# Reading and writing the fp32r products of a two-layer encoder from the last column to the first

## The chip, the cores and the metric

The kernel runs on one core of a Trainium2 chip. The metric is the device time of one execution in microseconds. It is measured in several runs, of which the median is given; a separate execution is taken with the hardware profiler.

## The reference: one step of a hybrid streaming encoder

Two layers work on a prompt of 2048 tokens and on 8 sample streams of 16 tokens, all with a model width of 1024 and in 32-bit floats.

```
p = rmsnorm(x) @ w_in[l]          # 1024 x 3584: mixer a | b | c | cross-attn q | gate
layer 0: softmax attention over the own chunk of 64 and 8 chunks before, with a bias by distance
layer 1: HGRN2 gated linear recurrence, state 128 x 128 for each of 6 heads
every layer: 4-head cross-attention into 256 memory tokens
y = concat(mixer_out, cross_out) * silu(gate);   x = x + y @ w_out[l]     # 1024 x 1024
final rmsnorm
```

Besides the two activations, the kernel returns the newest keys and values, the recurrent states and the memory keys and values. The largest part of the arithmetic is `rmsnorm(x) @ w_in[l]` for 2176 tokens, twice; then comes `y @ w_out[l]`.

## The kernel before, in words

**Products from high and low parts.** A plain fp32 product is one kind of matmul here, an fp32r product another. Where the kernel uses fp32r, it splits each operand into a high part (the value cast to fp32r) and a low part (the value minus its high part, again fp32r), and adds three products: weights' low by data's high, weights' high by data's high, weights' high by data's low.

**The input projection** (`project`, from L967; its tensor part is L1458 to L1480). The contraction over 1024 channels is cut into two halves of four blocks of 128, the output channels into pairs of groups of 128, and the tokens into two halves. Of these two-by-two blocks, seven sums or differences are formed (a scheme with seven products in place of eight), the *terms* j = 0 to 6. One term is 12 matmuls into one PSUM bank, `BANK[j]`: four of the weights' low part (L1464), then eight of the high part with the data's high and low parts in turn (L1468). The weights are the stationary operand (128 x 128), the data is the moving one. There are 14 column pairs of the weights, seven terms for each, and four passes over the tokens. A pass has 512 tokens, so the moving operand has 256 columns; the first pass also carries the 128 sample tokens, and its moving operand has 320. In layer 1, the first two column pairs of pass 0 are made with plain fp32 matmuls (L1459, four for a term).

TensorE goes through the steps in a fixed order written out by hand. Before a term it waits for the weights' low part from VectorE (`w.s_lo`), and for the bank to have been emptied (`s_cp`, `s_cb`). ScalarE makes the weights' high part (L509), VectorE the low part (L516); ScalarE copies (L1204, L1207) and VectorE combines (L1307) the banks into the output once the last matmul of a term has signalled `s_mm`. The weight terms of passes 1 to 3 are fetched again from memory by SyncE.

**The band attention of layer 0** (`prompt_band`, from L1927) works tile by tile on 128 tokens with plain fp32 matmuls for scores (L2321), transposes (L2352) and values (L2408). The output projection is woven between them by an inner function `project` (L2439 to L2455): for each tile and each half of 512 output columns it adds 8 x 3 fp32r matmuls (L2453). Here the data `yh`, `yl` is the stationary operand and the weights `woh`, `wol` are the moving one, with 512 columns.

**The recurrence of layer 1** (`prompt_hgrn`, from L2771) has the same output projection (L3032 to L3049), with its three products on lines L3043, L3044 and L3047, among plain fp32 products of 32 to 256 columns and transposes. A tile's 48 output products are given out in pieces between the levels of the recurrence.

Before the first projection stands `begin` (memory keys and values, with 64 plain fp32 matmuls of 512 columns at L942); between the recurrence and the second projection stands the sample streams' part. All moving operands and outputs of matmuls are read and written with a step of +1 column.

Of the kernel before, what the change touches and what calls it, by code (L numbers as in the profile page):

```python
# [22 lines left out]
KD = D // P  # L23
# [27 lines left out]
def place(step):  # L51
    p, r = divmod(step, STEPS)
    c, j = divmod(r, TERMS)
    return p, c, j
# [14 lines left out]
def made(step):  # L69

    return step + 1 - TERMS * place(step)[0]
# [34 lines left out]
def keep_going(nc, bank, ident, n):  # L106

    for _ in range(n):
        nc.tensor.transpose(bank[:, 0:P], ident[:], ident[:])
# [857 lines left out]
def project(nc, l, sem, ps_in, v, x, w, x_of, proj, keep, room, early, samp, opening):  # L967
# [30 lines left out]
    def pair(step):  # L998
        return step // TERMS
# [26 lines left out]
    with ExitStack() as ctx:  # L1026
# [18 lines left out]
        BANK = [B1[:], B52[:, 1], B4[:], B52[:, 0], B3[:], B76[:, 1], B76[:, 0]]  # L1045
# [26 lines left out]
        with nc.Block() as block:  # L1072
# [336 lines left out]
            @block.tensor  # L1409
            def _(pe):  # L1410
                def turn(i, kh):
                    pe.wait_ge(s_xn, i + 1)
                    if i or kh:
                        pe.wait_ge(x.s_raw, RAWS + 2 * i + kh)
                    elif l:
                        pe.wait_ge(x.s_raw, RAWS)
                        pe.wait_ge(s_rawa, len(ON_ACT))
                    for k in range(4):
                        at = (4 * kh + k) * P
                        ins = nc.tensor.transpose(TP[:, k * P:(k + 1) * P], nat[i % 2][:, at:at + P], ident[:])  # L1420
                    ins.then_inc(s_tp, 1)
                def first_turn(n):
                    i, kh = TURNS[n]
                    pe.wait_ge(early.s_xn, i + 1)
                    if n == 8:
                        pe.wait_ge(x.s_raw, 2)
                    if n == 9:
                        pe.wait_ge(x.s_raw, 3)
                    for k in range(4):
                        at = (4 * kh + k) * P  # L1430
                        ins = nc.tensor.transpose(SPACE[n % 8][:, k * P:(k + 1) * P], early.x[i][:, at:at + P], ident[:])
                    ins.then_inc(s_tp, 1)
                if l:
                    for n in range(len(TURNS)):
                        first_turn(n)
                    pe.wait_ge(x.s_raw, 5)
                    keep_going(nc, SPACE[3], ident, 9)
                for step in range(ALL):
                    p, c, j = place(step)
                    q, n = pair(step), x.width(p)  # L1440
                    if step < w.whole:
                        if j in w.PLAIN:
                            w.loaded(pe, c)
                        else:
                            w.summed(pe, c, j)
                        if c == 0 and j in x.SUMS:
                            pe.wait_ge(x.s_add, x.MADE[0][j])
                    else:
                        if not kept(step):
                            pe.wait_ge(w.s_lo, made(step) - w.whole)  # L1450
                        if c == (w.whole // TERMS if p == 0 else 0):
                            pe.wait_ge(x.s_lo, TERMS * p + (list(LOWS.values()).index(j) if l and p == 0 else j) + 1)
                    if j == 0 or j == 3:
                        wait(pe, s_cp, 3 * (q - 1) + (1 if j == 0 else 3))
                    if q and j:
                        pe.wait_ge(s_cb, 4 * (q - 1) + (2, 1, 2, 3, 4, 4)[j - 1])
                    if step < w.whole:
                        for k in range(4):  # L1458
                            ins = nc.tensor.matmul(BANK[j][:, 0:n], w.source(step)[:, k], x.source(0, j)[:, k],  # L1459
                                                   start=(k == 0), stop=(k == 3))  # L1460
                        ins.then_inc(s_mm, 1)
                        continue
                    for k in range(4):
                        ins = nc.tensor.matmul(BANK[j][:, 0:n], w.lo[j][:, k], x.of(x.hi, p, j)[:, k], start=(k == 0), stop=False)  # L1464
                    ins.then_inc(w.s_free, 1)
                    for k in range(4):
                        for i, y in enumerate((x.hi, x.lo)):
                            ins = nc.tensor.matmul(BANK[j][:, 0:n], w.hi[j][:, k], x.of(y, p, j)[:, k],  # L1468
                                                   start=False, stop=(k == 3 and i == 1))
                    ins.then_inc(s_mm, 1)  # L1470
                    if p < PASSES - 1 and c in (2, 4, 6, 8) and j in (1, 5):
                        turn(4 * p + c // 2 - 1, j // 4)
                if l == 0:
                    pe.wait_ge(x.s_raw, RAWS + 8 * (PASSES - 1))
                    keep_going(nc, TP, ident, 14)
# [451 lines left out]
def prompt_band(nc, l, sem, sb_in, sb_far_in, ps_in, v, early, opening):  # L1927
# [24 lines left out]
    with ExitStack() as ctx:  # L1952
# [3 lines left out]
        wol = sb("pb_wol", [P, KD, D], F32R)  # L1956
# [7 lines left out]
        woh = sb("pb_woh", [P, KD, D], F32R)  # L1964
# [17 lines left out]
        yh = [sb("pb_yh0", [P, KD, P], F32R), yh1]  # L1982
        with ExitStack() as over:
            y = [sb_in(over)("pb_y0", [P, KD, P]), y1]
        yl = [sb("pb_yl0", [P, KD, P], F32R), yl1]
# [34 lines left out]
        def group_of(T, p):  # L2020

            return p if T else (p - XP) % KD
# [25 lines left out]
        def sum_of(job, half):  # L2048

            return SC[0][:, 0:512] if (job, half) == (NT, 1) else OP[:]  # L2050
# [28 lines left out]
        with nc.Block() as block:  # L2079
# [168 lines left out]
            def _(pe):  # L2248
# [190 lines left out]
                def project(job, first, last):  # L2439

                    for n in range(first, last):
                        c, part = divmod(n, 3)
                        half, k = divmod(c, KD)
                        if part == 0 and k == 0 and (job, half) != (NT, 1):
                            wait(pe, s_xadd, 2 * job + half)
                        if part == 0 and k % 4 == 0:
                            pe.wait_ge(s_yh, 2 * job + k // 4 + 1)
                        if part == 2 and k % 4 == 0:
                            pe.wait_ge(s_yl, 2 * job + k // 4 + 1)
                        if job == 0 and part == 0 and half == 0:  # L2450
                            pe.wait_ge(s_wl, FIRST.index(group_of(0, k)) + 1)
                        cs = slice(half * 512, half * 512 + 512)
                        ins = nc.tensor.matmul(sum_of(job, half), (yl if part == 2 else yh)[job % 2][:, k],  # L2453
                                               (wol if part == 1 else woh)[:, group_of(job, k), cs],
                                               start=(k == 0 and part == 0), stop=(k == KD - 1 and part == 2))  # L2455
                        if k == KD - 1 and part == 2:
                            ins.then_inc(s_op, 1)
# [22 lines left out]
                for u in range(PAIRS, U_ALL, 2):  # L2480
                    T, p = step(u)
# [289 lines left out]
def prompt_hgrn(nc, l, sem, sb_in, ps_in, v, o_s, woh, wol, wor, ahead):  # L2771
# [19 lines left out]
    with ExitStack() as ctx:  # L2791
        sb, ps = sb_in(ctx), ps_in(ctx)
        q, f, k, tT, gt, xq, masks = ahead.q, ahead.f, ahead.k, ahead.vT, ahead.gate, ahead.xq, ahead.own
# [18 lines left out]
        y = [sb(f"hg_y{i}", [P, 512]) for i in range(2)]  # L2812
        yh = sb("hg_yh", [P, KD, P], F32R)
        yl = sb("hg_yl", [P, KD, P], F32R)
# [35 lines left out]
        def sum_of(job, half):  # L2850

            return SC[bank(NT - 1, LEVELS - 1)] if (job, half) == (JOBS - 1, 0) else OP
# [4 lines left out]
        with nc.Block() as block:  # L2857
# [100 lines left out]
            def _(pe):  # L2958
# [73 lines left out]
                def project(job, first, last):  # L3032

                    for c in range(first, last):
                        half, s = divmod(c, KD)
                        to = sum_of(job, half)
                        if s == 0:
                            wait(pe, s_xadd, 2 * job if job == JOBS - 1 else 2 * job + half)
                        if s % 4 == 0:
                            pe.wait_ge(s_yh, 2 * job + s // 4 + 1)  # L3040
                        cs = slice(half * 512, half * 512 + 512)
                        g = GROUPS[s]
                        nc.tensor.matmul(to[:], yh[:, s], woh[:, g, cs], start=(s == 0), stop=False)  # L3043
                        nc.tensor.matmul(to[:], yh[:, s], wol[:, g, cs], start=False, stop=False)  # L3044
                        if s % 4 == 0:
                            pe.wait_ge(s_yl, 2 * job + s // 4 + 1)
                        ins = nc.tensor.matmul(to[:], yl[:, s], woh[:, g, cs], start=False, stop=(s == KD - 1))  # L3047
                        if s == KD - 1:
                            ins.then_inc(s_op, 1)  # L3049

# [441 lines left out]
```

## Time and profile before

| what | value |
|---|---|
| median of 3 runs | 2377.52 us |
| lowest and highest | 2376.17, 2381.19 us |
| profiled execution, span from first to last instruction | 2376.1 us |
| PE (TensorE matmuls) busy | 2312.2 us, 97% |
| PEld (weight loads) busy | 2094.7 us, 88% |
| DVE (VectorE) busy | 1819.5 us, 77% |
| ACT (ScalarE) busy | 1413.5 us, 59% |
| POOL (GpSimd) busy | 381.0 us, 16% |
| matmuls | 23787 |
| mean granted TensorE clock | 0.997 |

For the profiled execution the span stands alone; the time around it isn't recorded separately. A matmul's recorded duration reaches from its start to its modelled end, and the next one starts before that end. So the rate of a stream of matmuls is read from the distance of their starts, not from their mean duration.

### The profile page before, as it was taken

The numbers are of one execution on the slowest core, as the hardware profiler recorded it, in microseconds if no ns is written. First come the engines' busy times: TensorE is split into PE (matmuls) and PEld (weight loads), VectorE is DVE, ScalarE is ACT, GpSimd is POOL, SyncE is SP. The second block draws the span as 40 slices with busy tenths as digits, with TensorE's granted clock in tenths as the row PEclk, the third lists the DMA queues.
The fourth block names the chain that finished last, engine by engine and source line by source line (L and its number), as shares of the span: only waits on it lengthen the run. The fifth ranks groups of instructions, "written<-read, shape, count | busy, mean of one in ns | idle before, by whom it ended". The sixth has DMA issues, their size and how long they took to land. (4 is left out here: it accounts for less than half of the span.)

```text
span 2376.1 us, 61711 instructions
## 1 busy us (share of the span) xinstructions
PE 2312.2 (97%) x23787; PEld 2094.7 (88%) x23787; DVE 1819.5 (77%) x3555; ACT 1413.5 (59%) x3281; POOL 381.0 (16%) x585
## 2 busy tenths in 40 slices
PE   7999999999989999999999999999999989999998
PEld 4999999999967888888887999999999978888886
DVE  7889788887666656666666998797888777888885
ACT  4564666755565555555554564776757566666664
POOL 2332000000022221211112332000000112112111
PEclk9999999999999999999999999999999999999999
DMA  6886887769894222222226897886879793444442
GB/s 227 298 299 219 301 281 231 247 220 332 232 307 121 83 66 89 90 69 83 73 81 232 272 303 242 256 275 214 266 248 312 230 269 117 129 131 122 137 135 70
DMA packets 396664, 469.64 MB, mean 198 GB/s; under 512 B 39860, under 2 KB 248556, under 8 KB 396376
## 3 DMA queue, kind: packets, MB, share of 16 engines
q1 hardware_dynamic: 379832, 406.02, 54.4%
q0 software_dynamic: 14704, 54.92, 6.6%
q10 hardware_dynamic: 1840, 4.75, 0.7%
q8 instruction: 193, 3.16, 0.5%
q14 instruction: 95, 0.78, 0.1%
HBM read 318.77 MB, written 151.56 MB: 198 GB/s over the span
## 5 line engine op out<-in xcount | busy, mean ns | idle before, releaser
L1468 PE MATMUL pj_acc<-x_lo,pj_wh 128*128 128x256 f32 (+1 forms) x3080 | 780.9, 284 | 0.0
L1468 PE MATMUL pj_acc<-x_hi,pj_wh 128*128 128x256 f32 (+1 forms) x3080 | 780.8, 284 | 0.0
L1468 PEld LDWEIGHTS pj_acc<-x_hi,pj_wh 128*128 128x128 f32 x3080 | 578.4, 188 | 0.0
L1468 PEld LDWEIGHTS pj_acc<-x_lo,pj_wh 128*128 128x128 f32 x3080 | 578.4, 188 | 0.0
L509 ACT ACTIVATE pj_wh<-pj_wt 128x512 fp32r<-128x512 f32 x676 | 420.3, 634 | 255.9 <-DMA pj_wt<-tsum 175.1
L516 DVE SCALAR_TENSOR_TENSOR pj_wl<-pj_wt,pj_wh 128x512 fp32r<-128x512 f32 x676 | 467.0, 708 | 87.0 <-ACT pj_wh L509 79.3
L1464 PE MATMUL pj_acc<-x_hi,pj_wl 128*128 128x256 f32 (+1 forms) x3080 | 509.4, 287 | 13.8 <-DVE pj_wl L516 11.9
L1464 PEld LDWEIGHTS pj_acc<-x_hi,pj_wl 128*128 128x128 f32 x3080 | 425.3, 188 | 22.1 <-DVE pj_wl L516 19.5
L1307 DVE TENSOR_TENSOR pj_out<-pj_out,pj_acc 128x512 f32<-128x512 f32 (+1 forms) x448 | 320.8, 716 | 103.3 <-PE pj_acc L1468 69.7
L2541 DVE COPY pb_pt<-pb_SCTP 128x256 f32<-128x256 f32 (+2 forms) x266 | 115.8, 435 | 147.5 <-PE pb_SCTP L2352 74.3
L2676 ACT ACTIVATE pb_se<-pb_se,pb_mn 128x640 f32<-128x640 f32 (+4 forms) x208 | 154.6, 745 | 114.6 <-DVE pb_mn L2524 114.3
L2683 ACT COPY pb_pt<-pb_SCTP 128x384 f32<-128x384 f32 (+2 forms) x272 | 106.3, 391 | 123.7 <-PE pb_SCTP L2356 62.9
L2524 DVE CUSTOM_DVE_ANT_0 pb_se<-pb_SCTP,pb_bias 128x640 f32<-128x640 f32 (+4 forms) x204 | 137.6, 727 | 44.0 <-PE pb_SCTP L2321 38.8
L2352 PE MATMUL pb_SCTP<-ident,pb_se 128*128 128x128 f32 x1020 | 156.9, 276 | 3.9 <-ACT pb_se L2676 2.6
L2352 PEld LDWEIGHTS pb_SCTP<-ident,pb_se 128*128 128x128 f32 x1020 | 121.5, 140 | 38.5 <-issue 9.2
L1204 ACT COPY pj_out<-pj_acc 128x512 f32<-128x512 f32 (+1 forms) x112 | 68.5, 611 | 115.5 <-PE pj_acc L1468 107.2
L1207 ACT COPY pj_out<-pj_acc 128x256 f32<-128x256 f32 (+1 forms) x224 | 85.4, 381 | 73.5 <-PE pj_acc L1468 69.7
L2453 PE MATMUL pb_OP<-pb_woh,pb_yh 128*128 128x512 f32 x264 | 127.1, 481 | 0.0
L2230 POOL TENSOR_TENSOR pb_gate<-pb_gate,pb_pt 128x128 f32<-128x128 f32 x136 | 74.9, 551 | 259.6 <-DVE pb_pt L2541 259.6
L3043 PE MATMUL hg_OP<-woh,hg_yh 128*128 128x512 f32 x264 | 115.5, 438 | 0.0
L478 POOL TENSOR_TENSOR pj_wt<-pj_wraw 128x512 f32<-128x512 f32 x56 | 89.1, 1594 | 120.4 <-PE pj_acc L1464 86.5
L2321 PEld LDWEIGHTS pb_SCTP<-pb_k,pb_q 64*128 64x128 f32 x1152 | 86.0, 187 | 23.9 <-issue 11.6
(371 smaller groups left out, 3992.1 us busy)
## 6 DMA issues: line engine op xcount, KB each, us to landing
pj_wt<-tsum SPq DMA_DIRECT2D x546, 256.0 KB, 3.8
proj<-pj_out SPq DMA_DIRECT2D x112, 512.0 KB, 4.2
tsum<-pj_wt SPq DMA_DIRECT2D x140, 256.0 KB, 3.2
pj_wraw<-in_w_in_dram POOLq DMA_DIRECT2D x24, 1024.0 KB, 6.6
tsum<-pj_wraw SPq DMA_DIRECT2D x56, 256.0 KB, 4.2
hg_x<-x_mid SPq DMA_DIRECT2D x17, 512.0 KB, 3.7
pb_gate<-proj SPq DMA_DIRECT2D x16, 512.0 KB, 5.1
pb_x<-in_x_prompt_dram SPq DMA_DIRECT2D x16, 512.0 KB, 3.8
```

The source lines that it names most:

```text
L509: nc.scalar.mul(self.hi[j][:], self.source(step), scale_of(column(step // TERMS), self.l)).then_inc(self.s_hi, 1)
L516: nc.vector.scalar_tensor_tensor(out=self.lo[j][:], in0=self.source(step), scalar=scale_of(column(step // TERMS), self.l), in1=self.hi[j][ ...
L1307: nc.vector.tensor_tensor(to, to, what, op).then_inc(s_cb, 1)
L1464: ins = nc.tensor.matmul(BANK[j][:, 0:n], w.lo[j][:, k], x.of(x.hi, p, j)[:, k], start=(k == 0), stop=False)
L1468: ins = nc.tensor.matmul(BANK[j][:, 0:n], w.hi[j][:, k], x.of(y, p, j)[:, k], start=False, stop=(k == 3 and i == 1))
L2352: ins = nc.tensor.transpose(to[:, at:at + P], se[u % 2][h][:, i * P:(i + 1) * P], ident[:])
L2453: ins = nc.tensor.matmul(sum_of(job, half), (yl if part == 2 else yh)[job % 2][:, k], (wol if part == 1 else woh)[:, group_of(job, k), cs] ...
L2524: nc.vector.tensor_tensor_reduce(se[u % 2][h][:, 0:n * P], scores_at(u, h, 0, n), add, 1.0, 3e38, ALU.add, ALU.min, mn[:, at:at + 1]).then ...
L2541: ins = nc.vector.tensor_copy(pt[u % 2][h][:, low * P:low * P + width], turned_to(u, h)[:, 512:512 + width])
L2676: nc.scalar.activation(se[u % 2][h][:, 0:n], src, ACT.Exp, bias=mn[:, at:at + 1], scale=-1.0, accum_out=tot[:, at:at + 1]).then_inc(s_exp, 1)
L2683: nc.scalar.copy(pt[u % 2][h][:, 0:at], turned_to(u, h)[:, 0:at]).then_inc(s_eva, 1)
L3043: nc.tensor.matmul(to[:], yh[:, s], woh[:, g, cs], start=(s == 0), stop=False)
```

## The change

In each fp32r product, the moving operand and the output get `::-1` on their columns. The column n - 1 is read first and written first to place n - 1 of the bank, column 0 last. The stationary operand, the order of the products, the waits and the signals are the same, and so are the plain fp32 products and transposes.

```diff
                     for k in range(4):
-                        ins = nc.tensor.matmul(BANK[j][:, 0:n], w.lo[j][:, k], x.of(x.hi, p, j)[:, k], start=(k == 0), stop=False)
+                        ins = nc.tensor.matmul(BANK[j][:, 0:n][:, ::-1], w.lo[j][:, k], x.of(x.hi, p, j)[:, k, ::-1], start=(k == 0), stop=False)
                     ins.then_inc(w.s_free, 1)
                     for k in range(4):
                         for i, y in enumerate((x.hi, x.lo)):
-                            ins = nc.tensor.matmul(BANK[j][:, 0:n], w.hi[j][:, k], x.of(y, p, j)[:, k],
+                            ins = nc.tensor.matmul(BANK[j][:, 0:n][:, ::-1], w.hi[j][:, k], x.of(y, p, j)[:, k, ::-1],
                                                    start=False, stop=(k == 3 and i == 1))
...
-                        ins = nc.tensor.matmul(sum_of(job, half), (yl if part == 2 else yh)[job % 2][:, k],
-                                               (wol if part == 1 else woh)[:, group_of(job, k), cs],
+                        ins = nc.tensor.matmul(sum_of(job, half)[:, ::-1], (yl if part == 2 else yh)[job % 2][:, k],
+                                               (wol if part == 1 else woh)[:, group_of(job, k), cs][:, ::-1],
                                                start=(k == 0 and part == 0), stop=(k == KD - 1 and part == 2))
...
-                        nc.tensor.matmul(to[:], yh[:, s], woh[:, g, cs], start=(s == 0), stop=False)
-                        nc.tensor.matmul(to[:], yh[:, s], wol[:, g, cs], start=False, stop=False)
+                        nc.tensor.matmul(to[:, ::-1], yh[:, s], woh[:, g, cs][:, ::-1], start=(s == 0), stop=False)
+                        nc.tensor.matmul(to[:, ::-1], yh[:, s], wol[:, g, cs][:, ::-1], start=False, stop=False)
                         if s % 4 == 0:
                             pe.wait_ge(s_yl, 2 * job + s // 4 + 1)
-                        ins = nc.tensor.matmul(to[:], yl[:, s], woh[:, g, cs], start=False, stop=(s == KD - 1))
+                        ins = nc.tensor.matmul(to[:, ::-1], yl[:, s], woh[:, g, cs][:, ::-1], start=False, stop=(s == KD - 1))
```

## Rows read from the trace of the kernel before

**Rows 1.** The page: span, busy times, busy tenths by slice, chain.

```profile
span 2376.1 us, 61711 instructions
PE 2312.2 (97%) x23787; PEld 2094.7 (88%) x23787; DVE 1819.5 (77%) x3555; ACT 1413.5 (59%) x3281; POOL 381.0 (16%) x585
...
PE   7999999999989999999999999999999989999998
...
PE hg_OP L3043 3%; PE hg_OP L3044 2%; PE hg_OP L3047 2%; PE hg_SC L2991 2%; PE hg_SC L3115 1%; PE hg_OB L3106 1%; PE hg_OB L3107 1%; PE hg_OB L3078 1%; PE hg_SC L3058 1%; PE hg_TP L3068 1%; PE hg_TP L3025 1%; PE hg_SC L3001 0%; PE hg_TP L3090 0%; PE hg_TP L3014 0%; PE hg_SC L2996 0%
```

**Rows 2.** Windows: us, then each engine's busy us and instructions, clock, DMA.

```profile
core 0: us, PE busy (x) PEld busy (x) DVE busy (x) ACT busy (x) POOL busy (x), PEclk, DMA share, GB/s
420.00:480.00 60.00, 60.00 (x532) 60.00 (x531) 49.74 (x81) 42.52 (x93) 5.64 (x4) 1.00 0.80 254
120.00:180.00 60.00, 60.00 (x415) 59.97 (x414) 52.94 (x76) 36.22 (x75) 21.09 (x18) 1.00 0.89 297
840.00:900.00 60.00, 60.00 (x562) 50.02 (x562) 36.14 (x94) 31.06 (x82) 12.44 (x29) 1.00 0.30 89
2220.00:2280.00 60.00, 59.23 (x1147) 49.17 (x1146) 48.68 (x122) 39.40 (x114) 13.42 (x19) 1.00 0.46 136
...
51.60:647.90 596.30, 591.59 (x4800) 587.43 (x4801) 482.11 (x721) 355.64 (x708) 73.03 (x65) 1.00 0.83 266
1283.90:1887.60 603.70, 595.46 (x4744) 581.97 (x4744) 521.50 (x788) 389.41 (x762) 66.68 (x62) 1.00 0.81 262
```

**Rows 3.** Groups by form, PE alone, windows 420:480 and 120:180.

```profile
L1420 PE MATMUL pj_tp<-ident,pj_nat 128*128 128x128 f32 x20 | 3.0, 272 | 0.0
...
L1420 PE MATMUL pj_tp<-ident,pj_nat 128*128 128x128 f32 x16 | 2.4, 272 | 0.0
```

**Rows 4.** Timeline of fp32r products: start us, duration us, engine, line, count.

```profile
100.12 0.75 PE L1464 MATMUL pj_acc<-x_hi,pj_wl 128*128 128x320 f32 x4
100.70 0.31 PE L1468 MATMUL pj_acc<-x_hi,pj_wh 128*128 128x320 f32 x1
...
501.36 0.62 PE L1464 MATMUL pj_acc<-x_hi,pj_wl 128*128 128x256 f32 x4
...
501.81 0.28 PE L1468 MATMUL pj_acc<-x_hi,pj_wh 128*128 128x256 f32 x1
...
2002.48 0.48 PE L3043 MATMUL hg_OP<-woh,hg_yh 128*128 128x512 f32 x1
2002.80 0.40 PE L3044 MATMUL hg_OP<-wol,hg_yh 128*128 128x512 f32 x1
...
2003.27 0.40 PE L3043 MATMUL hg_OP<-woh,hg_yh 128*128 128x512 f32 x1
2003.50 0.40 PE L3044 MATMUL hg_OP<-wol,hg_yh 128*128 128x512 f32 x1
2003.74 0.40 PE L3047 MATMUL hg_OP<-woh,hg_yl 128*128 128x512 f32 x1
```

**Rows 5.** Waits of PE in the two projections: total us, times, longest us.

```profile
PE pj_acc L1464 <- DVE pj_wl L516: 4.4, 10, 1.5
...
PE pj_acc L1464 <- DVE pj_wl L516: 7.5, 12, 1.5
```

**Rows 6.** Groups by form, whole span: the changed products with their counts.

```profile
L1468 PE MATMUL pj_acc<-x_hi,pj_wh 128*128 128x256 f32 x2352 | 564.5, 277 | 0.0
...
L1464 PE MATMUL pj_acc<-x_hi,pj_wl 128*128 128x256 f32 x2352 | 369.9, 279 | 3.8 <-DVE pj_wl L516 3.3
...
L1468 PE MATMUL pj_acc<-x_hi,pj_wh 128*128 128x320 f32 x728 | 216.3, 309 | 0.0
...
L2453 PE MATMUL pb_OP<-pb_woh,pb_yh 128*128 128x512 f32 x264 | 127.1, 481 | 0.0
...
L3044 PE MATMUL hg_OP<-wol,hg_yh 128*128 128x512 f32 x264 | 104.3, 395 | 0.5 <-issue 0.5
```

**Rows 7.** Timeline of plain fp32 products and transposes.

```profile
27.19 12.18 PE L942 MATMUL bg_kv<-bg_wkvb,bg_xT 128*128 128x512 f32 x28
...
1286.22 2.05 PE L1459 MATMUL pj_acc<-x_raw,pj_wt 128*128 128x320 f32 x7
...
2001.69 1.04 PE L3068 MATMUL hg_TP<-ident,hg_se 128*128 128x128 f32 x8
```

## The prediction

> **What bounds the kernel now.** I began with the page's first two parts [rows 1]: PE is busy for 2312.2 of 2376.1 us (97%), DVE for 77%, ACT for 59%, and PE's row of slices shows 9 in nearly all of them. Since matmuls are pipelined and their ends are modelled, that share alone doesn't show that PE is at its peak, so the next view is the busy time by windows [rows 2]. Of 60 us in the later passes of the first projection, PE shows 60.00 and issues 532 matmuls. The list by form for that window gives 20 of them as transposes [rows 3]. At 0.109 us each (below) these take 2.2 us, so the other 512 start every 57.8 / 512 = 0.113 us. The timeline shows the same without averaging: four products from 501.36 to 501.81, 0.1125 us each [rows 4]. A product of 320 columns, in a projection's first pass, starts every (100.70 - 100.12) / 4 = 0.145 us; by the window at 120 us, (60 - 16 x 0.109) / 399 = 0.146 us [rows 2 to 4]. A product of 512 columns in an output projection starts 0.23 to 0.24 us after the one before (2003.27, 2003.50, 2003.74) [rows 4]. So in the two projections, 596.3 and 603.7 us long [rows 2], PE is fed all the time: it idles for 596.3 - 591.6 = 4.7 and 603.7 - 595.5 = 8.2 us there, nearly all of it for the low part that DVE makes [rows 5]. The band attention stage also shows PE at 60.00 of 60, and the recurrent stage at 59.23 [rows 2]. The chain that ended last, as far as the page follows it, consists of PE work, with the three output product lines at its head [rows 1]. TensorE's granted clock is 1.00 in these stretches, the level of 2.4 GHz. Every nanosecond added to a changed product is therefore paid nearly in full.
>
> **The change part by part.** Nothing is added, removed or moved: 10,824 matmuls keep their place, size, stationary operand, waits and increments. 7056 of them have 256 columns (2352 at L1464, two times 2352 at L1468), 2184 have 320 (three times 728), 1584 have 512 (three times 264 at L2453, and 264 each at L3043, L3044, L3047) [rows 6]. Two things differ per product: the order in which the columns of the moving operand are read, and the order in which the results are written. Both are turned the same way, so each value lands where it landed, and the vector and scalar engines read the banks as before. They start when the last product of a term has ended, so which column came last is nothing to them. The next product into the same bank also runs backwards, so the time between two accumulations into one column stays one interval. At equal rate the sum is 10,824 x 0 = 0.
>
> The price of a backward stream is in no row, since every pattern here goes forward. The nearest rows bound it. *Upper end:* a changed product moves one column in 0.113 / 256 = 0.44 ns, against 1 / 2.4 = 0.42 ns for a column per clock. The plain fp32 products take twice that: 28 products of 512 columns in 12.18 us, less the last one's 0.59, are 11.59 / 27 = 0.429 us each, and seven of 320 columns in 2.05 us, less 0.43, are 0.270 us, so 0.84 ns per column. Even a 128-column fp32 transpose takes (1.04 - 0.27) / 7 = 0.109 us, which is 0.85 ns per column [rows 7]. So the fp32r stream moves two neighbouring columns in the time that the plain one needs for one. If the pairing worked only upwards, 256 columns would take 0.215 us, 320 0.270, 512 0.429. That is 7056 x 0.102 = 720 us, 2184 x 0.124 = 271 us, 1584 x (0.429 - 0.232) = 312 us; sum 1303 us, less the 12.9 us that PE idles in the projections and would no longer: +1290 us. *Lower end:* a changed product has a remainder over its columns at 0.417 ns: 6.2 ns at 256, 12.7 at 320 (146 - 133.3), 18.7 at 512 (232 - 213.3). The plain ones have about 2 ns (109 - 106.7 at 128; 429.3 - 426.7 = 2.6 at 512). Were the surplus of about 4, 10 and 16 ns due to the direction, turning it round could give back 7056 x 4 + 2184 x 10 + 1584 x 16 ns = 28 + 22 + 25 = 75 us, and no more.
>
> I take zero. Both numbers of the bounds belong to something that the direction doesn't touch by necessity: a backward stream still asks for neighbours one after the other, the counts 256, 320 and 512 are even, so the pairs (255, 254), (253, 252), ... are the very pairs of the forward stream, and each lies in the same aligned 8 bytes. I choose the nearest row, the same product forward.
>
> The trace has the forward rate of 0.44 ns per column for unit steps alone [rows 4]. The Trainium skill (Advanced Engine Details and Errata, PSUM Cachelines) has the results' memory work in lines of two FP32 values, and says that every two consecutive elements should be contiguous, but also that any non-contiguous pattern significantly slows down matmuls. By its first half the reversed write costs nothing (each line is met twice in a row), and the sum is 0; read to the letter, a step of -1 is not a contiguous pattern, which speaks against this change, and the sum is at the upper end. No run yet shows which. The same page (VectorE Performance Modes) counts +1 and -1 alike as unit step for that engine; no row here shows a step of -1 on any.
>
> What is hidden if the upper end holds: DVE and ACT would have more time per term, and the waits for the low part would go; nothing else could cover PE, which has no other idle time.
>
> **The rivals.**
>
> *Pairing only upwards* (slower). Place: every fp32r product, on the read or the write side, one being enough. Price: as above, 2377.5 + 1290 = 3667 us. It decides as soon as the pair's address is formed by adding to the first rather than by recognising the line. For it: fp32r is visibly a special fast path, twice the plain rate [rows 4, 7], and special paths tend to have narrow conditions. Against it: the pairs are aligned and their members adjacent in time.
>
> *A small cost or loss per product* (slower). The path works backwards, but each stream loses something at its start, or the surplus of 4, 10 and 16 ns doubles: between 10,824 x 0.44 ns = 4.8 us, from where it can be told, and 75 us: 2382 to 2453 us. One period at 1.2 GHz, 0.83 ns, per product would be 9 us, 2386 us. For it: what happens around a product's start does cost something: the first 512-column product after plain fp32 ones is followed after 0.32 us instead of 0.23 (2002.48 to 2002.80) [rows 4]. Against it: that price is one of changing the kind of product, which stays as it is.
>
> *The surplus shrinks* (faster). If forward streams lose their 4 to 16 ns to meeting the weight loads' reads, which run all the time in the projections (PEld 60.00 of 60 in the window at 420 us [rows 2]), a backward one may meet them less: down to 2377.5 - 75 = 2302 us. For it: the surplus grows with the columns and the plain products lack it. Against it: nothing says that the direction matters.
>
> *The change does nothing* because both turns cancel before they reach the engine, as the instruction could be given forward with the same meaning. The time is then 2377.5 us and cannot be told from my forecast by time.
>
> **How the numbers follow.** The sum is 0 on the profiled execution's span of 2376.1 us; the median of the runs, 2377.52, lies 1.4 us above it and the runs spread from 2376.17 to 2381.19. I forecast 2377.5 us. About 0.2%, 4.8 us, is what a measurement of this kernel can tell from no change. Chances: no difference 58% (54 for equal rate, 4 for a change without effect), pairing only upwards 19%, a small cost 14%, the surplus shrinking 9%. So faster 9%, same 58%, slower 33%. A range from 2310 to 2455 us holds the first, the small cost and most of the gain, 81% in all; it leaves out the 19% at 3667 us.
>
> **What would show it.** Right: the 256-column products again start 0.113 us apart, 320 at 0.146, 512 at 0.23, and the window inside the first projection again holds about 532 matmuls in 60 us. Pairing only upwards would show at once: starts 0.215 us apart, PE full, DVE and ACT waits longer, the projections about 500 us longer each. A small cost shows in the same intervals by its nanoseconds, in equal amounts at 256, 320 and 512 if it is one per product, in proportion to the columns if it lies in the stream. The forecast is wrong if the intervals of plain products stay at 0.109 and 0.429 us while those of the changed ones move.

## The result: 1.1% slower, and the profile after

| what | before | after |
|---|---|---|
| median | 2379.36 us (4 runs, 2376.17 to 2381.20) | 2408.01 us (4 runs, 2403.61 to 2412.39) |
| ratio after to before | | 1.011, 95% interval 1.0087 to 1.0133 |
| span of the profiled execution | 2376.1 us | 2403.1 us |

The page of the changed kernel, span and busy times; it answers to [rows 1]:

```profile
span 2403.1 us, 61711 instructions
PE 2340.1 (97%) x23787; PEld 2125.0 (88%) x23787; DVE 1824.5 (76%) x3555; ACT 1417.3 (59%) x3281; POOL 379.5 (16%) x585
```

PE is busy 28 us longer. The busy times by window, for the stretches of [rows 2] (columns as there; the projections' windows follow their first and last product):

```profile
420.00:480.00 60.00, 60.00 (x507) 60.00 (x506) 46.45 (x76) 42.20 (x93) 5.63 (x4) 1.00 0.79 238
120.00:180.00 60.00, 60.00 (x416) 59.98 (x415) 53.00 (x77) 36.29 (x75) 20.31 (x17) 1.00 0.89 296
...
51.10:661.10 610.00, 607.56 (x4800) 604.72 (x4801) 483.72 (x721) 356.96 (x708) 72.33 (x65) 1.00 0.82 260
1295.90:1913.70 617.80, 609.36 (x4744) 596.94 (x4744) 526.14 (x788) 391.83 (x762) 65.97 (x62) 1.00 0.81 256
```

The two projections last 610.0 and 617.8 us instead of 596.3 and 603.7. That is 27.8 us, the whole loss (27.0 us of span). At the same granted clock, 60 us of a later pass hold 507 matmuls where they held 532. The first pass, with 320 columns, holds 416 against 415: nothing changed there.

The timeline of the changed kernel shows the pace, and something that I had overlooked before. These are the first four products of each term (L1464, one row each) with the transposes (L1420) between; the L1468 rows are left out:

```profile
414.99 0.64 PE L1464 MATMUL pj_acc<-x_hi,pj_wl 128*128 128x256 f32 x4
416.43 0.64 PE L1464 MATMUL pj_acc<-x_hi,pj_wl 128*128 128x256 f32 x4
417.87 0.64 PE L1464 MATMUL pj_acc<-x_hi,pj_wl 128*128 128x256 f32 x4
419.30 0.60 PE L1420 MATMUL pj_tp<-ident,pj_nat 128*128 128x128 f32 x4
419.66 0.72 PE L1464 MATMUL pj_acc<-x_hi,pj_wl 128*128 128x256 f32 x4
421.15 0.63 PE L1464 MATMUL pj_acc<-x_hi,pj_wl 128*128 128x256 f32 x4
422.57 0.63 PE L1464 MATMUL pj_acc<-x_hi,pj_wl 128*128 128x256 f32 x4
423.98 0.63 PE L1464 MATMUL pj_acc<-x_hi,pj_wl 128*128 128x256 f32 x4
```

A term of twelve products takes 1.44 us before the transposes (416.43 to 417.87: 0.120 us a product) and 1.41 us behind them (422.57 to 423.98: 0.118 us). The kernel before has two paces as well, and there too an interruption changes them. Its timeline:

```profile
250.29 0.63 PE L1464 MATMUL pj_acc<-x_hi,pj_wl 128*128 128x256 f32 x4
251.70 0.63 PE L1464 MATMUL pj_acc<-x_hi,pj_wl 128*128 128x256 f32 x4
253.11 0.64 PE L1464 MATMUL pj_acc<-x_hi,pj_wl 128*128 128x256 f32 x4
254.53 0.60 PE L1420 MATMUL pj_tp<-ident,pj_nat 128*128 128x128 f32 x4
254.89 0.72 PE L1464 MATMUL pj_acc<-x_hi,pj_wl 128*128 128x256 f32 x4
256.35 0.62 PE L1464 MATMUL pj_acc<-x_hi,pj_wl 128*128 128x256 f32 x4
257.71 0.62 PE L1464 MATMUL pj_acc<-x_hi,pj_wl 128*128 128x256 f32 x4
259.07 0.62 PE L1464 MATMUL pj_acc<-x_hi,pj_wl 128*128 128x256 f32 x4
```

1.41 us a term (0.118) before the transposes, 1.36 us (0.113) behind them. So a stream of these products settles into a repeating pattern and, in most stretches, keeps it until a transpose or a wait breaks in. Distance by distance, the kernel before runs in 113, 113, 114 ns (mean 113.3) most of the time and in one of mean 117.7 for the rest; the changed one in 115, 118, 120 (mean 117.8) or in a steady 120. Of its 588 terms in passes 1 to 3, none has the fast pattern; of those of the kernel before, 499 have it (mean under 114 ns over products 3 to 11).

Over all 7056 products of 256 columns (each start to PE's next start): those under 130 ns were 6972 with a mean of 114.00 ns, 794.8 us in all, and are 7000 with a mean of 118.56 ns, 829.9 us. The longer ones, waits and restarts, went from 84 with 25.8 us to 56 with 16.5 us. Together +25.8 us. At 4.56 ns more for each of the 7056 it would have been 32.2 us, so 6.4 us were covered by fewer and shorter waits.

### The profile page after: what moved, and what is told of

The parts are those of the page before. It is cut to its first block and busy times, and to the rows that moved or that the text cites. A ratio compares the mean times of both kernels' runs of the same rounds, so it can differ in the third digit from the quotient of the medians.

```text
span 2403.1 us, 61711 instructions
## 1 busy us (share of the span) xinstructions
PE 2340.1 (97%) x23787; PEld 2125.0 (88%) x23787; DVE 1824.5 (76%) x3555; ACT 1417.3 (59%) x3281; POOL 379.5 (16%) x585
## 5 line engine op out<-in xcount | busy, mean ns | idle before, releaser
L1468 PE MATMUL pj_acc<-x_lo,pj_wh 128*128 128x256 f32 (+1 forms) x3080 | 801.3, 289 | 0.0
L1468 PE MATMUL pj_acc<-x_hi,pj_wh 128*128 128x256 f32 (+1 forms) x3080 | 801.1, 289 | 0.0
L1468 PEld LDWEIGHTS pj_acc<-x_hi,pj_wh 128*128 128x128 f32 x3080 | 579.3, 188 | 0.0
L1468 PEld LDWEIGHTS pj_acc<-x_lo,pj_wh 128*128 128x128 f32 x3080 | 579.2, 188 | 0.0
L1464 PE MATMUL pj_acc<-x_hi,pj_wl 128*128 128x256 f32 (+1 forms) x3080 | 519.1, 291 | 11.7 <-DVE pj_wl L516 9.7
L1464 PEld LDWEIGHTS pj_acc<-x_hi,pj_wl 128*128 128x128 f32 x3080 | 433.0, 188 | 18.0 <-DVE pj_wl L516 15.7
L2676 ACT ACTIVATE pb_se<-pb_se,pb_mn 128x640 f32<-128x640 f32 (+4 forms) x208 | 154.6, 745 | 114.0 <-DVE pb_mn L2524 113.7
L1204 ACT COPY pj_out<-pj_acc 128x512 f32<-128x512 f32 (+1 forms) x112 | 68.4, 611 | 122.1 <-PE pj_acc L1468 114.0
L3043 PE MATMUL hg_OP<-woh,hg_yh 128*128 128x512 f32 x264 | 116.1, 440 | 0.0
L2221 POOL COPY pb_rb<-pb_rs 128x128 f32<-128x128 f32 x136 | 41.1, 302 | 417.9 <-DVE pb_rs L2530 417.8
```

The costliest lines, as they stand in the source:

```text
L1464: ins = nc.tensor.matmul(BANK[j][:, 0:n][:, ::-1], w.lo[j][:, k], x.of(x.hi, p, j)[:, k, ::-1], start=(k == 0), stop=False)
L1468: ins = nc.tensor.matmul(BANK[j][:, 0:n][:, ::-1], w.hi[j][:, k], x.of(y, p, j)[:, k, ::-1], start=False, stop=(k == 3 and i == 1))
L2676: nc.scalar.activation(se[u % 2][h][:, 0:n], src, ACT.Exp, bias=mn[:, at:at + 1], scale=-1.0, accum_out=tot[:, at:at + 1]).then_inc(s_exp, 1)
L3043: nc.tensor.matmul(to[:, ::-1], yh[:, s], woh[:, g, cs][:, ::-1], start=(s == 0), stop=False)
```

## The experiments

One table for all. "In 60 us" is the number of matmuls that the profile counts in the window from 420 to 480 us of the profiled execution (532 in the kernel before, 507 in the changed one). "Mean" is that of the start distances under 130 ns of the 256-column products of passes 1 to 3; "fast" is the share of distances under 115 ns among them. Both are worked out from all starts in the trace. Where no ratio stands, the time is a single run, beside one of the kernel before on the same chip. Each "mean" and "fast" comes from one execution. How much they vary by themselves shows in e2_out_proj, whose 256-column products are those of the kernel before, and in e4_write: 114.7 ns and 70 to 71% against 114.0 ns and 85%.

| kernel | time | in 60 us | mean | fast |
|---|---|---|---|---|
| before | 2379.36 us | 532 | 114.0 ns | 85% |
| changed | 1.011 (1.0087 to 1.0133) | 507 | 118.6 | 0% |
| e1_in_proj | 1.0098 (1.0075 to 1.0121) | 507 | 118.6 | 0% |
| e2_out_proj | 1.0017 (1.0003 to 1.0032) | 531 | 114.7 | 71% |
| e3_read | 1.0093 (1.0074 to 1.0113) | 508 | 118.8 | 0% |
| e4_write | 0.9993 (0.9981 to 1.0005) | 531 | 114.7 | 70% |
| e5_shift | 1.0094 (1.0072 to 1.0116) | 510 | 117.8 | 23% |
| e6_pairs | 1.0103 (1.0081 to 1.0126) | 511 | 118.0 | 0% |
| e7_lines_back | 1.0098 (1.0073 to 1.0123) | 511 | 118.1 | 0% |
| e8_inside_back | 1.0006 (0.9992 to 1.0020) | 531 | 114.2 | 82% |
| e9_half_fwd | 2384.67, before 2380.94 us | 531 | 114.5 | 77% |
| e10_half_back | 2404.00, before 2380.94 | 511 | 118.2 | 0% |
| e11_sweep_back | 2403.23, before 2380.94 | 511 | 118.5 | 0% |
| e12_sweep_fwd | 2398.98, before 2380.94 | 515 | 117.2 | 25% |
| e13_shift_both | 2388.30, before 2382.00 | 526 | 115.6 | 52% |
| e14_sweep_back2 | 2406.39, before 2382.00 | 509 | 118.8 | 1% |
| e15_alternate | 2402.98, before 2382.00 | 513 | 117.8 | 8% |
| e16_same_weight_fwd | 2395.10, before 2382.56 | 526 | 116.1 | 39% |
| e17_same_weight_back | 2402.03, before 2382.56 | 514 | 117.8 | 0% |
| e18_blocks32 | 2405.25, before 2382.56 | 513 | 117.7 | 3% |

### Where: which products, and which side

The two halves of the change were run apart; then, in the input projections, the read alone and the write alone:

```diff
# e3_read
+ ... matmul(BANK[j][:, 0:n],           w.hi[j][:, k], x.of(y, p, j)[:, k][:, ::-1], ...
# e4_write
+ ... matmul(BANK[j][:, 0:n][:, ::-1],  w.hi[j][:, k], x.of(y, p, j)[:, k], ...
```

> Only the input projections' fp32r products (L1464, L1468) run backwards; the output projections run forward. Theory: the whole loss lies in the 256-column products, whose starts moved from 0.113 us to 0.118 or 0.120 us apart, so this kernel loses the full 26 us (2400 to 2412 us). Rival, a cost in every changed product or in the output projections: a clearly smaller loss, below 20 us.

> Only the output projections' products of 512 columns (L2453, L3043, L3044, L3047) run backwards. Theory: same as before within 3 us, starts at 0.231 to 0.236 us as before. Rival (the output projections carry a part): 5 us or more.

> In the input projections only the moving operand is read backwards, the results are written forward, so the columns of each product arrive mirrored; the output differs from the reference's. Theory A, the loss comes from the read, which meets the weight loads' reads at other addresses: 118 to 120 ns intervals at 256 columns and 20 to 30 us lost. Theory B, it comes from the write into the bank: 113 ns as before, 0 us. Theory C, it takes both turns: 0 us here and in the kernel that turns only the write.

> In the input projections only the result is written backwards, the moving operand is read forward; the output differs from the reference's. Theory A (read): 0 us, 113 ns intervals. Theory B (write): 20 to 30 us and 118 to 120 ns. Theory C (both needed): 0 us.

The input projections alone lose 0.98%, as much as the change within its uncertainty. The output projections alone come to 1.0017, about 4 us, between what I had given for the theory (3 us at most) and for the rival (5 us or more). The sums of their start distances say little: 431.1 us for the 512-column products in e2_out_proj, 428.7 before, 428.1 in the changed kernel. But a product that stands between two others of 512 columns is followed after 233.5 ns in e2_out_proj and in the changed kernel, and after 232.6 to 232.9 ns in the 18 kernels that run them forward; of those forward distances 86 to 106 in some 855 are under 230 ns, of the backward ones none. So a backward product of 512 columns costs a little under 1 ns, 1 to 2 us over all of them. The rest of e2's 4 us isn't explained by the edit: in its trace the untouched 256-column products sum to 4.9 us more back-to-back time than in that of the kernel before, the variation named above the table. The read alone loses 0.93%, the write alone nothing (0.9993). The write direction is free in these products, and the read is what costs. The busy times of e3_read and then of e4_write in the window at 420 us:

```profile
420.00:480.00 60.00, 60.00 (x508) 60.00 (x506) 45.82 (x75) 42.52 (x96) 5.63 (x4) 1.00 0.78 237
```

```profile
420.00:480.00 60.00, 60.00 (x531) 60.00 (x530) 49.64 (x80) 42.40 (x93) 5.65 (x4) 1.00 0.81 256
```

### What of it: the order inside 16 bytes, the order of larger blocks, or the place

Two kernels keep some of the reversal: pairs and groups of four columns go down through the tile while the order inside them is ascending. One does the opposite. In a fourth nothing is reversed, but the tiles of passes 1 to 3 lie 252 columns further on; only ring slots 0 to 6 have room for that, slots 7 and 8 stay.

```diff
# e6_pairs (b=2), e7_lines_back (b=4); the output likewise
+ x.of(y, p, j)[:, k].rearrange("p (a b) -> p a b", b=4)[:, ::-1]
# e8_inside_back
+ x.of(y, p, j)[:, k].rearrange("p (a b) -> p a b", b=4)[:, :, ::-1]
# e5_shift, in Halves.of
- ...rearrange("p k n -> p (k n)")[:, 0:4 * HALF]
+ ...rearrange("p k n -> p (k n)")[:, 252:252 + 4 * HALF]
```

> Everything runs forward, but in passes 1 to 3 the data tiles are kept 252 columns (1008 bytes) further on in their buffers, so each forward stream of 256 columns begins at nearly the address at which the backward stream of the changed kernel begins. Theory 'direction' (what counts is that the read now goes the same way as the weights' read): like before, mostly 113.3 ns, 0 to 5 us. Theory 'start address' (the first column's place decides): mostly 118 to 120 ns, 20 to 30 us slower.

> Input projections only; read and write go backward by pairs of columns, forward within a pair (254, 255, 252, 253, ...). Theory 'direction': the stream still descends through the buffer, so 118 to 120 ns at 256 columns, 20 to 30 us slower. Theory 'pairing' (the fast path wants an ascending pair): 113.3 ns mostly, 0 to 5 us. If it costs a multiple, a jump between pairs has a price of its own.

> Input projections only; read and write go backward by groups of four columns (16 bytes), forward within a group. Theory 'direction': 118 to 120 ns, 20 to 30 us slower. Theory 'pairing' or 'order within 16 bytes': 113.3 ns mostly, 0 to 5 us.

> Input projections only; the groups of four columns follow each other forward, inside a group the four are read and written backward. Theory 'direction': the stream ascends, 113.3 ns mostly, 0 to 5 us. Theory 'order within 16 bytes': 118 to 120 ns, 20 to 30 us slower.

The windows at 420 us of e7_lines_back and then of e8_inside_back:

```profile
420.00:480.00 60.00, 60.00 (x511) 60.00 (x510) 46.49 (x76) 42.74 (x96) 5.63 (x4) 1.00 0.77 239
```

```profile
420.00:480.00 60.00, 60.00 (x531) 60.00 (x531) 49.73 (x80) 42.96 (x95) 5.64 (x4) 1.00 0.81 250
```

The order inside 16 bytes doesn't matter (e8: 1.0006), the order of the 16-byte groups does (e7: 1.0098). The theory that a fast path needs an ascending pair falls with e6, which has such pairs and is slow, and with e8, which has none and is fast. But e5_shift was a surprise for "direction": it reads forward all the time and loses 0.94%. Its timeline, term by term, with the L1468 rows left out; by the kernel's ring the first four terms use slots 3 to 6, which were moved, and the fifth and sixth use slots 7 and 8, which were not:

```profile
549.88 0.64 PE L1464 MATMUL pj_acc<-x_hi,pj_wl 128*128 128x256 f32 x4
551.31 0.64 PE L1464 MATMUL pj_acc<-x_hi,pj_wl 128*128 128x256 f32 x4
552.74 0.64 PE L1464 MATMUL pj_acc<-x_hi,pj_wl 128*128 128x256 f32 x4
554.17 0.64 PE L1464 MATMUL pj_acc<-x_hi,pj_wl 128*128 128x256 f32 x4
555.60 0.63 PE L1464 MATMUL pj_acc<-x_hi,pj_wl 128*128 128x256 f32 x4
556.97 0.62 PE L1464 MATMUL pj_acc<-x_hi,pj_wl 128*128 128x256 f32 x4
558.33 0.40 PE L1464 MATMUL pj_acc<-x_hi,pj_wl 128*128 128x256 f32 x2
```

1.43 us for a term of a moved slot (551.31 to 552.74; 0.119 us a product), 1.37 and 1.36 us for the unmoved ones (0.114). Over passes 1 to 3 of layer 0 the moved slots have means of 119.2 to 119.3 ns, the unmoved ones 114.1 and 114.3. The place of a tile sets the pace of its own products.

### Place against what? And has the backward read a good place?

`e11` and `e12` give each of the slots 0 to 6 another offset; `e14` is a second set. `e13` moves the weights' tiles and the data's slots 0 to 6 by the same 32 bytes.

```diff
# Halves.of, e11_sweep_back and e12_sweep_fwd (columns of 4 bytes)
+ at = (4, 8, 16, 32, 64, 128, 240)[(TERMS * p + j) % self.SLOTS]
+ return whole.rearrange("p k n -> p (k n)")[:, at:at + 4 * HALF]...
# e13_shift_both: at = 8, and
- sb0("pj0_shift", [P, 16])
+ sb0("pj0_shift", [P, 24])
# the same for pj1_shift0 and pj1_shift1, and pj1_pad1 496 -> 488
```

> All products of the input projections run backwards. In passes 1 to 3 the data tiles of ring slots 0 to 6 begin 16, 32, 64, 128, 256, 512 and 960 bytes further on in their buffers, one offset for each slot; slots 7 and 8 stay. Theory 'relative address' (what counts is where the moving stream starts against where the weight load starts, not the direction): the interval differs by slot, slots 7 and 8 stay at 118 to 120 ns, and at least one offset brings 113.3 ns. Rival 'direction': all nine slots at 118 to 120 ns.

> The same seven offsets with all products forward. Theory 'relative address': slots 7 and 8 at 113.3 ns, several of the seven moved slots at 117 to 123 ns, so 10 to 25 us slower. If all nine slots stay at 113.3 ns, the loss of the earlier kernel with an offset of 1008 bytes had another cause.

> Forward. The weights' tiles lie 32 bytes further on in both layers, and in passes 1 to 3 so do the data tiles of ring slots 0 to 6; slots 7 and 8 stay. Theory 'place of the data against the weights': slots 0 to 6 are back at 113.3 ns (an offset of 32 bytes for the data alone gave 118.0), slots 7 and 8, whose data stayed while the weights moved, go to 116 to 120 ns. Rival 'place of the data alone': slots 0 to 6 at 118 ns, slots 7 and 8 at 113.3 ns.

> All products of the input projections backward; ring slots 0 to 6 at offsets of 48, 96, 160, 192, 320, 384 and 448 bytes in passes 1 to 3. Theory 'every direction has its favourable place': one of the seven at 113 to 115 ns. Rival 'the backward read has a floor of its own': all at 117.8 to 120 ns, as the eight offsets tried so far.

The mean distance by slot in the first projection (products 3 to 11 of each term, waits left out):

| bytes | 0 | 16 | 32 | 64 | 128 | 256 | 512 | 960 |
|---|---|---|---|---|---|---|---|---|
| forward (e12) | 114.7 to 115.2 | 118.9 | 118.0 | 118.8 | 117.8 | 116.9 | 115.6 | 119.0 |
| backward (e11) | 117.8 | 120.0 | 117.8 | 118.1 | 119.7 | 117.8 | 117.8 | 119.8 |

| bytes | 0 | 48 | 96 | 160 | 192 | 320 | 384 | 448 |
|---|---|---|---|---|---|---|---|---|
| backward (e14) | 117.8 | 119.7 | 117.8 | 119.6 | 119.9 | 118.2 | 119.9 | 120.2 |

Forward, sixteen bytes away from the place that the kernel before uses, the products take 118.9 ns. Backward the place matters too (117.8 or about 120 ns), but there is no good one among the fifteen: none lies below 117.8 ns. All fifteen are multiples of 16 bytes; no run tries others. So in e11 the theory of the relative address was right that the slots would differ and wrong that one of them would bring 113.3 ns.

The timeline of e13_shift_both, one row for the start of each term and the others left out, slots 5, 6, 7, 8, 0 and 1 in turn:

```profile
387.26 0.62 PE L1467 MATMUL pj_acc<-x_hi,pj_wl 128*128 128x256 f32 x4
388.62 0.62 PE L1467 MATMUL pj_acc<-x_hi,pj_wl 128*128 128x256 f32 x4
389.98 0.63 PE L1467 MATMUL pj_acc<-x_hi,pj_wl 128*128 128x256 f32 x4
391.39 0.63 PE L1467 MATMUL pj_acc<-x_hi,pj_wl 128*128 128x256 f32 x4
392.80 0.64 PE L1467 MATMUL pj_acc<-x_hi,pj_wl 128*128 128x256 f32 x4
394.19 0.62 PE L1467 MATMUL pj_acc<-x_hi,pj_wl 128*128 128x256 f32 x4
395.55 0.62 PE L1467 MATMUL pj_acc<-x_hi,pj_wl 128*128 128x256 f32 x4
```

Slots 5 and 6, moved along with the weights, take 1.36 us (0.113 a product). Slots 7 and 8, which stayed while the weights moved, take 1.41 us (0.117). Slot 0 needs its first products to find the pattern again (1.39 us), slot 1 is back at 1.36. With the data moved by 32 bytes alone, e12 had 118.0 ns. Over passes 1 to 3 of layer 0, slots 1 to 6 have means of 114.0 to 115.1 ns (113.7 to 114.5 in the kernel before), slot 0 behind the two unmoved ones 115.8, slots 7 and 8 117.7 and 117.9. So what counts is the data's place against the weights'. Without the 64 bytes of `pj0_shift`, `pj1_shift0` and `pj1_shift1` the data would lie 64 bytes further on against the weights, where e12 has 118.8 ns; so these tiles probably put the place right for a forward read. No run takes them away.

### Is it the weight load?

Six more kernels. In two of them, seven of the eight L1468 products of a term load half the weight columns. In two, the load reads one column 128 times. One reads backward and forward in turn, and one has longer ascending blocks:

```diff
# e9_half_fwd; e10_half_back with ::-1 on moving and output
+ m = P if (k, i) == (3, 1) else P // 2
+ matmul(BANK[j][0:m, 0:n], w.hi[j][:, k, 0:m], x.of(y, p, j)[:, k], ...
# e16_same_weight_fwd; e17_same_weight_back with ::-1 on moving and output
+ matmul(BANK[j][:, 0:n], w.hi[j][:, k][:, 0:1].to_broadcast([P, P]), x.of(y, p, j)[:, k], ...
# e15_alternate
+ matmul(BANK[j][:, 0:n][:, ::1 - 2 * i], w.hi[j][:, k], x.of(y, p, j)[:, k][:, ::1 - 2 * i], ...
# e18_blocks32: as e7, with b=32
```

> Forward; seven of the eight products of a term at L1468 load only 64 of the 128 weight columns and fill 64 of the 128 output rows (the other half of those sums is left out). Theory 'the moving read meets the weight read': with half the weight reads the remainder over the columns' 106.7 ns shrinks, intervals at or below 111 ns. If the weight load plays no part: 113.3 ns as before.

> As the one before, with read and write backwards; the same half of the sums is left out. Theory 'the moving read meets the weight read': clearly below 118 ns, nearly as the forward one. Rival (the backward read is slow by itself, whatever the weights do): 118 to 120 ns remain.

> At L1468 the products with the data's low part run backward and those with its high part forward, in turn; L1464 forward. Theory 'each backward product costs its own': the mean over a forward and a backward one lies half way, 115.5 to 117 ns. Rival 'the hand-over from one stream to the next': either all pairs as slow as or slower than all-backward, or as fast as all-forward.

> Forward, and the weight load reads the block's first column 128 times instead of 128 columns, so every output row of the input projections gets the sum of one channel; the weights' read no longer walks. Theory 'the two walks meet': without one of them the interval is the same in both directions, near or below 113.3 ns here. Rival 'the backward read is slow by itself': 113.3 ns here.

> The same with read and write backward. Theory 'the two walks meet': the interval of the forward twin within 1 ns. Rival 'the backward read is slow by itself': 117.8 to 120 ns.

> Input projections; blocks of 32 columns (128 bytes) follow each other backward, forward within a block. Blocks of 2 and 4 columns gave 117.8 to 120 ns. Theory 'what counts is the place at each moment': with 32 columns most of each block is read in ascending order, but its place against the weights is another one, so neither 113.3 nor 118 to 120 exactly; I expect 115 to 121 ns. If it is 113.3 ns, the ascending run of 32 is enough and place is secondary.

The groups of e9_half_fwd in the window at 420 us (busy us, mean ns of one) show that the load did get shorter, by 54 ns:

```profile
L1469 PEld LDWEIGHTS pj_acc<-x_hi,pj_wh 128*64 128x64 f32 x170 | 22.8, 134 | 0.0
L1464 PEld LDWEIGHTS pj_acc<-x_hi,pj_wl 128*128 128x128 f32 x171 | 22.6, 188 | 0.0
```

The pace hardly changed: 114.5 ns forward, 118.2 backward. How long the weights are read is not what sets it, and my expectation for both kernels was wrong. Loading one column again and again changed the patterns, but the backward read stayed at 117.8 ns. The first rows of four terms in the timeline of e17_same_weight_back:

```profile
549.68 0.63 PE L1464 MATMUL pj_acc<-x_hi,pj_wl 128*128 128x256 f32 x4
551.10 0.63 PE L1464 MATMUL pj_acc<-x_hi,pj_wl 128*128 128x256 f32 x4
552.51 0.63 PE L1464 MATMUL pj_acc<-x_hi,pj_wl 128*128 128x256 f32 x4
553.92 0.63 PE L1464 MATMUL pj_acc<-x_hi,pj_wl 128*128 128x256 f32 x4
```

1.413 us a term, 117.8 ns a product, in all 588 terms; the steady 120 ns is gone, the fast pattern didn't come. Its forward twin wandered between 113, 116 and 120 ns with a mean of 116.1, which neither theory had foreseen; 227 of its 588 terms have the fast pattern. So the theory that the loss is the meeting of two walks falls: without the weights' walk the backward read did no better than 117.8 ns, while the forward one still reached 113.3 in places. The steady 120 ns came backward only where the weights' read walks.

Alternating came to 117.8 ns, above the 115.5 to 117 that I had given for "each its own": the L1468 products take 118.0 ns in the mean, close to the 118.6 of the changed kernel, and no term has the fast pattern. One backward read in two is enough to lose it.

Blocks of 32 columns, 128 bytes of ascending read each, take 117.7 ns in the mean, within the 115 to 121 that I had expected, but not everywhere. In 19 of the 588 terms, in five stretches that each begin with a start distance of 196 to 222 ns, e18_blocks32 has the fast pattern; in none of the other kernels that read all columns, pairs or groups of four downwards does a term have it. The first rows of four terms in a row, 1.36 us apart, from its timeline:

```profile
631.60 0.62 PE L1464 MATMUL pj_acc<-x_hi,pj_wl 128*128 128x256 f32 x4
...
632.96 0.62 PE L1464 MATMUL pj_acc<-x_hi,pj_wl 128*128 128x256 f32 x4
...
634.32 0.62 PE L1464 MATMUL pj_acc<-x_hi,pj_wl 128*128 128x256 f32 x4
...
635.68 0.62 PE L1464 MATMUL pj_acc<-x_hi,pj_wl 128*128 128x256 f32 x4
```

So descending blocks don't exclude the fast pattern once they are 128 bytes long; they make it rare. Blocks between 16 and 128 bytes weren't tried.

**What stays open.** Why the fast pattern never comes with a read that goes down by up to 16 bytes at a time, why it came now and then with 128 bytes, and by what the pace locks. No run turns the weight load round as well, so whether two descending reads would get on is not known.

## Why the prediction was wrong

- **What bounds the kernel: right.** PE paced by the starts of the fp32r products. Of the 32.2 us that the slower pace costs, 25.8 us were paid and 6.4 us absorbed by fewer and shorter waits. I had put the absorbable idle time at 12.9 us.
- **"I take zero" failed, and the step was this one: "a backward stream still asks for neighbours one after the other ... I choose the nearest row, the same product forward."** The mechanism looked at a product by itself, its pairs and its 8 bytes. That part held: order inside 16 bytes is free (e8), the write side is free (e4), and nothing fell to half rate. What it put at nothing was the step from one product to the next: the reversed read made the 256-column products start 118.56 ns apart instead of 114.00. The 0.113 us was not the property of a product. It is one of several patterns into which a train of products and weight loads settles. With a forward read it comes at the right spacing, with a fully reversed one it came in none of 588 terms. The trace before had the sign of it: 0.118 us for a stretch of the same products with the same form, at 250 us. I averaged over a window that had none of it and took its figure for the rate. The small tiles named "shift" and "pad" beside the weights' tiles in the code were a second sign, which I didn't follow up. That the measured 2408 us lies in the range of 2310 to 2455 us is no merit of this step: the range was wide for the sake of the rivals.
- **No row gave a price: half right.** The bounds of -75 and +1290 us held the result. The lower one was built from the remainder over 0.417 ns a column. For 256 columns that remainder grew from 7.3 to 11.9 ns in the mean (114.0 and 118.56 less 106.7), while 320 columns kept theirs (146.7 ns in both kernels) and 512 gained under 1 ns (232.7 and 233.5). I had all three move together. The count was short, too: 48 products of 512 columns stand in other rows than those I counted (8 x 3 in the band attention write pb_SCTP, 8 x 3 in the recurrence write hg_SC), so 10,872 products change. At the upper bound that is 9 us more.
- **Pairing only upwards: refuted** by e6 and e8; e8 has every pair descending and loses nothing. The Trainium skill (Advanced Engine Details and Errata, SBUF Cachelines) has accesses that hit the same 16-byte cacheline run at full performance; e8, which changes the order inside 16 bytes alone, agrees with 1.0006. The order of the 16-byte groups costs 0.98% in e7. The sentence of the Trainium skill (Advanced Engine Details and Errata, PSUM Cachelines) by which any non-contiguous pattern slows matmuls down doesn't bear on a reversed write here: e4 stands at 0.9993.
- **A small cost per product: the nearest rival, at 14%, with the right size (2382 to 2453 us) and the wrong cause.** It is neither the same for each product nor in proportion to its columns: 4.6 ns at 256 columns, nothing that shows at 320, under 1 ns at 512.
- **The surplus shrinks: wrong sign,** though its reason, the weight loads beside the read, was half of the story: the place against the weights matters (e13), the length of the load does not (e9).
- **The change does nothing: excluded** by the time.

## What to carry to other kernels

When a kernel's pace is set by a dense train of matmuls with a weight load each, look at the start distances one by one, over several stretches, before calling any of them the rate; more than one value for the same form means that a pattern is at work, and that a change of address, direction or interruption can flip it. A spacing between tiles that suits one order of access need not suit another: after a change of read order, sweep the spacing again, which ring slots with different offsets allow in a single run. Here the sweep found no place that gives the loss back. And a control inside the same kernel, slots that are not moved, tells more than many timed rounds.

## What the runs showed of the hardware that I had not expected

- fp32r products of 256 columns, each with its weight load, settle at 113.3, 117.7 or 120.0 ns from start to start at a granted clock of 1.00 in the kernels before and after, and mostly change only where a transpose or a wait breaks in. A column for each period at 2.4 GHz would be 106.7 ns.
- Moving the read operand by 16 bytes against the weights takes the mean to 118.9 ns, where the unmoved slots of the same run have 114.7 to 115.2. Moving both by 32 bytes leaves slots 1 to 6 at 114.0 to 115.1 ns.
- Reading the moving operand downwards by single columns, pairs or groups of four gave no term below 117 ns, with single columns at fifteen places, all multiples of 16 bytes, and with a weight load that is shorter or reads one column only. With blocks of 32 columns the mean is 117.7 ns, but 19 of 588 terms ran at 113.3. Writing the result downwards is free (0.9993).
- Products of 320 columns show no dependence on direction (146.7 ns both ways), those of 512 columns a small one (232.7 to 233.5 ns). Why these differ from the 256-column ones is open.
